# A decoder layer on one core: one gate eviction and three weight sums moved to earlier places in their engines' queues

## The reference

```
xn   = rms_norm(x)
proj = xn @ w_in               # q, k, v of both mixers, their gates, and gate_pre
ya   = diff_attention(...) @ w_proj_a
yb   = mlstm(...)          @ w_proj_b
g    = sigmoid(gate_pre)       # two branch gates of width 1024
h    = x + (g[0] * ya + g[1] * yb) @ w_out
u    = relu(rms_norm(h) @ w_ff1)         # 1024 x 4096
h    = h + (u * u) @ w_ff2               # 4096 x 1024
out  = rms_norm(h)
```

## Time and profile before

| | us |
|---|---|
| median of 3 runs | 1906.81 (1903.93 to 1907.09) |
| the profiled execution's own time | 1905.65 |
| its span from first to last instruction | 1903.7 |
| PE busy | 1887.6 |
| DVE busy | 1204.3 |
| ACT busy | 948.4 |
| POOL busy | 334.5 |

### The profile page before, as it was taken

One profiled execution on the slowest core, in us unless ns is written; L12 is line 12 of the kernel. 1 busy time (PEld: TensorE's weight loads), 2 busy tenths in 40 slices (PEclk: granted clock), 3 DMA queues, 4 the chain that ended last, 5 costly groups with the idle time before them and its releaser, 6 DMA issues. The chain is left out here.

```text
span 1903.7 us, 26951 instructions
## 1 busy us (share of the span) xinstructions
PE 1887.6 (99%) x9960; PEld 1618.5 (85%) x9960; DVE 1204.3 (63%) x1560; ACT 948.4 (50%) x1541; POOL 334.5 (18%) x182
## 2 busy tenths in 40 slices
PE   9999999999999999999999999999999999999998
PEld 6989898989898989888888888878888888888887
DVE  7675758576767676644311122687778778789774
ACT  5455655556555655445333322237576585333343
POOL 2202020211111110232123444420000000121002
PEclk9999999999999999999999999999999999999999
DMA  5341515151424242432254444557677577454422
GB/s 213 112 155 67 177 56 193 51 197 50 175 66 151 87 159 83 165 106 72 75 191 150 140 141 171 179 182 265 206 258 274 200 277 234 184 224 147 147 83 89
DMA packets 103283, 292.86 MB, mean 154 GB/s; under 512 B 10889, under 2 KB 28041, under 8 KB 92193
## 3 DMA queue, kind: packets, MB, share of 16 engines
q1 hardware_dynamic: 100896, 283.36, 43.1%
q10 hardware_dynamic: 2304, 8.39, 1.1%
HBM read 204.61 MB, written 87.10 MB: 153 GB/s over the span
## 5 line engine op out<-in xcount | busy, mean ns | idle before, releaser
L753 PE MATMUL gp<-r1h,w_hi 128*128 128x512 f32 x880 | 346.7, 394 | 1.2 <-ACT ev L1146 1.2
L755 PE MATMUL gp<-r1h,w_lo 128*128 128x512 f32 x880 | 343.5, 390 | 0.0
L754 PE MATMUL gp<-r1l,w_hi 128*128 128x512 f32 x880 | 342.7, 389 | 0.0
L1034 PE MATMUL scores<-xh,qh 128*128 128x512 f32 x512 | 200.4, 391 | 3.0 <-ACT res L1417 2.1
L1038 PE MATMUL scores<-xh,ql 128*128 128x512 f32 x512 | 199.3, 389 | 0.0
L1036 PE MATMUL scores<-xl,qh 128*128 128x512 f32 x512 | 199.2, 389 | 0.0
L755 PEld LDWEIGHTS gp<-r1h,w_lo 128*128 128x128 f32 x880 | 165.2, 188 | 35.2
L753 PEld LDWEIGHTS gp<-r1h,w_hi 128*128 128x128 f32 x880 | 165.3, 188 | 34.3 <-issue 1.6
L754 PEld LDWEIGHTS gp<-r1l,w_hi 128*128 128x128 f32 x880 | 165.4, 188 | 32.2
L1263 ACT ACTIVATE pr<-scores,nb 128x256 f32<-128x256 f32 (+7 forms) x128 | 93.7, 737 | 117.1 <-DVE nb L1686 117.1
L2058 POOL TENSOR_TENSOR w_lo<-w_raw,w_hi 128x1024 fp32r<-128x1024 f32 x25 | 60.5, 2421 | 508.4 <-ACT w_hi L1137 486.2
(11 more groups left out here) (351 smaller groups left out, 4312.7 us busy)
## 6 DMA issues: line engine op xcount, KB each, us to landing
xraw<-xo_d SPq DMA_DIRECT2D x54, 1024.0 KB, 5.2
w_raw<-in_in_blocks SPq DMA_DIRECT2D x64, 512.0 KB, 3.7
proj_d<-ev SPq DMA_DIRECT2D x128, 256.0 KB, 2.2
rq<-in_ff_quarters SPq DMA_DIRECT2D x32, 1024.0 KB, 7.9
xo_d<-res SPq DMA_DIRECT2D x78, 256.0 KB, 3.2
xo_d<-ring SPq DMA_DIRECT2D x60, 256.0 KB, 3.0
gt<-proj_d SPq DMA_DIRECT2D x32, 256.0 KB, 3.3
xt<-in_x_halves SPq DMA_DIRECT2D x8, 512.0 KB, 7.2
```

The lines of the kernel that those rows point to most:

```text
L753: pe.matmul(gp[half][:], wh[slot][:, k, :], mh[:, k, t], start=(k == 0), stop=False)
L754: pe.matmul(gp[half][:], wh[slot][:, k, :], ml[:, k, t], start=False, stop=False)
L755: mm = pe.matmul(gp[half][:], wl[slot][:, k, :], mh[:, k, t], start=False, stop=(k == KT - 1))
L1034: pe.matmul(bank, qh[s % 3][:, k, cols], xh[s % 3][:, k, :], start=first and k == 0, stop=False, skip_group_check=True)
```

## The change

In the gate stretch the eviction of unit 2 goes from the head of slot 1 to ACT's slot 0, behind the high part of the third block. In the feed-forward loop sum 3 of a group goes from idx 1 of its own group to idx 6 of the group ahead (group 0 keeps it at stage 1), and sums 1 and 2 go from idx 5 and 6 of the group ahead to idx 4 and 5. The three now stand behind the low parts of their iteration, where they stood ahead of them.

```diff
                 for k in GATE_UNITS_AT[s]:
-                    evac(N_GATE + k // 2, k % 2)
-                attend(NH - 1, s, lambda: None, None, lambda: split_hi(N_GATE + 2, (N_GATE + 2) // 2, 0))
+                    if k != 2:
+                        evac(N_GATE + k // 2, k % 2)
+
+                def third_unit():
+                    split_hi(N_GATE + 2, (N_GATE + 2) // 2, 0)
+                    evac(N_GATE + 1, 0)
+
+                attend(NH - 1, s, lambda: None, None, third_unit)
...
                     if 1 <= g <= GROUPS and idx == 1:
                         hidden_turned(g - 1, 3)
-                    if idx == 1:
-                        weight_sum(g, 3)
+                    if s == 1:
+                        weight_sum(0, 3)
                     if idx == 3 and g:
                         weight_sum(g, 4)
-                    if g < 2 * GROUPS - 1 and idx in (5, 6):
-                        weight_sum(g + 1, idx - 4)
                     if s + 2 < STAGES:
                         q_lo_part(s + 2)
                         x_lo_part(s + 2)
+                    if g < 2 * GROUPS - 1 and idx in (4, 5, 6):
+                        weight_sum(g + 1, idx - 3)
                     if 1 <= g <= GROUPS and idx == 0:
                         for u in range(3):
                             hidden_turned(g - 1, u)
```

## The result

The changed kernel takes 1916.27 us (median of 5 runs, 1914.85 to 1917.85), the kernel before, run beside it, 1904.85 us (5 runs, 1903.93 to 1907.09). The ratio is 1.0057, with a 95% interval of 1.0042 to 1.0072: slower by 11.4 us. The prediction was wrong: it said 1908.7 us, with 1904 to 1910.5 as its own range and 1914 as the edge of the widest. One execution of the third experiment's kernel took 8355 us and is left out of its ratio. The lines of the changed kernel are six higher than those of before from the gates on: L1417 is L1423, L1845 is L1851, L1927 is L1933.

The account below looks back on a forecast made before the run. PE was taken as the bound, busy 1887.6 of 1903.7 us. Terms -1.4 - 3.1 + 6.4 = +1.9 us on 1905.65 gave 1907.6, and 1908.7 against the median; own range 1904 to 1910.5, widest 1901.6 to 1914.

Parts of the forecast that it names:

- The gate part: In the gates, PE's wait at 817 for the eviction of unit 2 goes: -1.4 us, bounds -1.4 and 0.
- What the feed-forward part removes: Groups 1 to 4, idx 2: PE's four waits for ACT's read-out L1417, behind sum 3, go: -3.1 us.
- Idx 5 and 6: Sums moved ahead of `add_bank`: PE's first unit of idx 6 still gets its bank in time, by 0.26 us; costed at nothing.
- rival D: Group 5: POOL's products fall elsewhere and the 0.7 us waits for DVE go, up to -1.9 us; no chance given.
- The chain to the new stop: Groups 1 to 4: `hidden_turned` 4.4 us later, so x, quarter 0 and the awaited `res` store land late; PE stops at idx 3.
- The failed step: PE's new stop at the first unit of idx 3, groups 1 to 4: +6.4 us, bounds nothing to 18.8 us.
- rival B: Store lands 9 us or more after x; stop of 3 us or more per group, +12 us and above, 1914 and more; chance 0.12.

Follow-up runs that it names:

- third experiment: Changed kernel with sums 1 and 2 back at idx 5 and 6, and sum 3 at idx 6 behind the four `add_bank`: 1901.65 us, ratio 0.9976.
- fifth: Changed kernel with sum 2 behind the four `add_bank` of idx 5 instead of ahead of them: 1902.19 us, ratio 0.9985.
- sixth: Changed kernel with sum 3 behind the `add_bank` of idx 6, sum 2 still ahead of those of idx 5: 1904.32 us, ratio 0.9992.
- fourth: Changed kernel with quarter 0's load behind the four stores of `hidden_turned` u = 3 in SP's queue: 1903.53 us, ratio 0.9987.
- seventh: Changed kernel with the four stores of u = 3 ahead of both loads in SP's queue at idx 1, groups 1 to 4: 1916.91 us, ratio 1.0057.
- eighth: The third experiment's kernel with quarter 0's load also behind the stores of u = 3 in SP's queue: 1900.07 us, ratio 0.9973.

## Why the prediction was wrong

**The gate part: right.** 1.4 us forecast, 1.3 us at the place, and nothing queued behind. Alone it measures 0.9991.

**What the feed-forward part removes: right.** The four stops in the middle of idx 2 and ACT's wait for sum 3 are gone.

**Idx 5 and 6: right.** The first matmul of idx 6 follows without a stop, with 0.1 us of slack in groups 0 to 3. Group 5's waits are 0.8 and 0.7 us, so rival D fell.

**The chain to the new stop: right in each link.** The forecast is first, the measured number in brackets; the group starts 0.2 us later in the profile after. `hidden_turned` 14.0 us into the group (13.97), x issued at 1370.8 (1370.49), the quarter 0.4 us behind (0.5), x landing at 1376.6 (1376.2), the quarter at 1379.0 (1379.1), and the awaited store behind both.

**The failed step is the size of that term.** It read "So PE stops there for 1.7 us" and "The other three groups I take as like group 1, a little lower, 1.6 us each: +6.4 us". Measured were 2.48 us in group 1 and 11.8 in all. Two things were too small. The store landed 2.7 us after the quarter, not the 1.9 us read off a place where x was issued 4.4 us ahead of the quarter and landed 0.5 us behind the store's issue: +0.8. And the other groups are not like group 1 and a little lower but higher: in group 2 x is issued 23.7 us into the group instead of 23.1 and takes 6.3 us instead of 5.7, so the store lands 35.3 us into it instead of 34.4.

```profile
1449.90 0.38 SPq L641 DMA_DIRECT2D xraw<-xo_d  x1
...
1451.48 0.46 SPq L649 DMA_DIRECT2D xo_d<-res  x1
```

```profile
xraw<-xo_d SPq DMA_DIRECT2D x1, 1024.0 KB, 6.3
...
xo_d<-res SPq DMA_DIRECT2D x1, 256.0 KB, 10.0
```

Group 2 starts at 1426.19. The profile of before could have told me to look, since its four groups took 33.49 to 34.15 us with waits that differ; I read one. The Trainium skill, "DMA: Bandwidth & Descriptors", section "Anatomy of one DMA", gives its figures for the path of transfers that GpSimd issues, while these are issued by SP. The landing estimated from it was 1380.2, with 1381.8 measured; the rows were nearer, and too early still. Two slips carry no weight: 1.7 and three times 1.6 make 6.5, not 6.4, and one wait of PE, 0.5 us for DVE's L1822 at 1257.7, lies outside the start of the kernel, where the prediction put all that it didn't list.

**A term was missing: the clock.** Two of the stops were each followed by about 3.4 us at the 1.2 GHz level, which cost 3.3 us together. The prediction priced a stop at its length, for the 1.2 us stops of before showed nothing else. The Trainium skill, "TensorE: Matmul & The Clock Gate", Part 1: The HAM clock gate, says that the default state is the throttled one, of 1.2 GHz, and that activity releases it. The window at 1462.2 agrees with the level. For stops as short as these the rows decide: in groups 1 to 4 of all runs none under 2.6 us was followed by it. The profile of before had one row that speaks of it: from 7.6 to 11.9 us PE ran nothing but matmuls of 4 columns, and from 12.3 to 15.8 us the granted clock was 0.51 (in the profile of the third experiment it stayed at 1.00 there). With stops of up to 4.7 us in its range, the prediction should have had the clock there too.

6.4 forecast, +5.4 of stops, +3.3 of clock and 0.4 of remainder make the 15.5 of the account. In size this is rival B, with a stop of some 3 us and +12 us, at a chance of 0.12. Its own words were off, too: it asked for a store landing 9 us or more after x, but here the store came 5.6 us after x in group 1 and the loss was there already. By the prediction's own working (1.7 us of stop for 4.3 us after x) a stop of 3 us needs only 5.6. So the point from which B decides lay close to the forecast, and its chance should have been larger.

**What is shown, what not.** That sums 2 and 3 ahead of `add_bank` cause the loss by making `hidden_turned` late is shown by the third, fifth and sixth experiments; that it passes through the quarter's load ahead of the store, by the fourth; that x is the next bound, by the seventh. Why the clock falls behind one stop and not behind another a little longer stays open.

## What to carry to other kernels

Before work is put earlier on an in-order engine, look for a hole where that engine waits; ahead of the work that others wait for, two such instructions made `hidden_turned` late by both their lengths (4.4 us), and behind that work the last one cost nothing: here 0.9976 against 1.0057 for the same three sums. A small awaited store can land with the prefetches ahead of it in the queue (9.9 us here, 3.1 without them), so take its landing from a place with as many loads ahead, and for every group, not the first. And where a forecast adds stops of 2 to 3 us to a TensorE that runs without gaps, put the clock into the range.

## What the runs showed of the hardware

In groups 1 to 4 the awaited 256 KB store took 2.9 to 3.2 us to land with no load just ahead of it (seventh experiment), 7.9 to 8.4 us behind one of 1 MB (fourth and eighth) and 9.8 to 10.2 us behind two (the changed kernel; 8.9 to 10.3 us over all runs with that order). The two loads themselves, where issued 0.5 us apart, took 5.7 to 7.1 and 7.9 to 9.2 us.

After stops of 2.65, 2.97, 3.20, 3.25, 3.29, 3.38 and 3.80 us TensorE ran for about 3.4 us at the 1.2 GHz level, which cost 1.4 to 1.6 us each time; after stops of 2.03, 2.48, 2.72, 2.80 and 3.04 us, and after all those of up to 1.5 us, it did not. The fall came between 0.3 us before and 1.4 us after the first matmul behind the stop. A longer stop was followed by it more often, but its length alone does not order these.
